# Moving two activation tensors by 128 and 384 bytes in SBUF, with everything behind them 512 bytes lower

## The reference, cut to what matters

```python
for layer in range(DEPTH):                       # first stack
    x = x + 0.5 * swiglu_ffn(rms_norm(x, ffn1_norm[layer]), w_gu, w_down)
    x = x + (even_mixer if layer % 2 == 0 else odd_mixer)(rms_norm(x, mix_norm[layer]), ...)
    x = x + memory_cross_attention(rms_norm(x, xa_norm[layer]), rms_norm(mem, ...), ...)
    x = x + 0.5 * swiglu_ffn(rms_norm(x, ffn2_norm[layer]), w_gu, w_down)
for l in range(DEPTH):                           # second stack
    x = x + 0.5 * rmsnorm(swiglu(rmsnorm(x, w_pre), w_gu, w_down), w_post)
    x = x + rmsnorm(merged(diff_attention, mlstm) @ w_out, w_mix_post)
    x = x + 0.5 * rmsnorm(swiglu(...), w_post)
```

## The kernel before, in words

| tensor | before | remainder by 256, by 512 | after | remainder by 256, by 512 |
|---|---|---|---|---|
| raw | 16512 | 128, 128 | 16512 | 128, 128 |
| a | 33056 | 32, 288 | 32928 | 160, 160 |
| b | 49696 | 32, 32 | 49312 | 160, 160 |
| x | 66272 | 224, 224 | 65760 | 224, 224 |
| score | 141024 | 224, 224 | 140512 | 224, 224 |
| hmid | 161568 | 32, 288 | 161056 | 32, 288 |
| w_hi | 163680 | 96, 352 | 163168 | 96, 352 |
| w_lo | 188256 | 96, 352 | 187744 | 96, 352 |

## Time and profile before

### The profile page before, as it was taken

The page is one execution under the profiler, slowest core; times in us unless marked ns, Lnnn a source line. Parts: engine busy times, 40 slices in busy tenths (PEclk is TensorE's granted clock), DMA queues, the critical chain, the costliest instruction groups (busy, mean ns, idle before and its releaser), DMA issues.

```text
span 2668.7 us, 51716 instructions
## 1 busy us (share of the span) xinstructions
PE 2587.6 (97%) x18604; PEld 2380.8 (89%) x18604; DVE 1919.6 (72%) x3131; ACT 1502.3 (56%) x2579; POOL 202.0 (8%) x280
## 2 busy tenths in 40 slices
PE   8999799999999999999999999999999999999998
PEld 7998689999999799999998998989989989988997
DVE  7777676778777586777777667777787776676876
ACT  6556556556555656556555555655565565555554
POOL 0001001000000101000000170000000004300000
PEclk9999899999999999999999999999999999999999
DMA  7654244665554254554654553445545545435553
GB/s 265 205 189 135 79 143 144 231 204 185 190 189 158 96 166 138 186 188 165 206 188 136 190 163 105 158 158 189 189 158 189 188 143 174 135 114 171 174 189 110
DMA packets 122821, 445.80 MB, mean 167 GB/s; under 512 B 13688, under 2 KB 14712, under 8 KB 122688
## 3 DMA queue, kind: packets, MB, share of 16 engines
q1 hardware_dynamic: 120816, 436.79, 49.4%
q0 software_dynamic: 1872, 7.17, 0.7%
HBM read 442.86 MB, written 1.05 MB: 166 GB/s over the span
## 4 chain that ended last, share of the span: by engine, by line
PE 92%; DVE 5%; ACT 2%; issue 1%; DMA 0%; SPq 0%; DVEq 0%; ACTq 0%
PE bank L459 91%; DVE w_lo L1473 1%; PE bank L810 1%; DVE rt L1701 1%; DVE z L1539 1%; ACT w_hi L1039 0%; DVE rt L1495 0%; DVE x L1532 0%; DVE a L1500 0%; ACT score L1273 0%; DVE rstd_x L1492 0%; DMA x<-in_x_dram 0%; ACT L1247 0%; DMA raw<-in_stream_dram 0%; DVE z L1645 0%
## 5 line engine op out<-in xcount | busy, mean ns | idle before, releaser
L459 PE MATMUL bank<-a,w_hi 128*128 128x256 f32 (+1 forms) x5360 | 1329.9, 328 | 40.6 <-DVE a L1500 37.9
L1473 DVE TENSOR_TENSOR w_lo<-raw,w_hi 128x1024 fp32r<-128x1024 f32 x829 | 1014.1, 1227 | 279.0 <-ACT w_hi L1039 278.6
L459 PE MATMUL bank<-a,w_lo 128*128 128x256 f32 x3736 | 1008.7, 281 | 0.0
L459 PEld LDWEIGHTS bank<-a,w_hi 128*128 128x128 f32 x5360 | 890.1, 190 | 130.7 <-issue 46.7
L1039 ACT CAST w_hi<-raw 128x1024 fp32r<-128x1024 f32 x829 | 858.3, 1047 | 40.5 <-DMA raw<-in_stream_dram 37.2
L459 PE MATMUL bank<-b,w_hi 128*128 128x256 f32 (+1 forms) x4096 | 845.0, 299 | 4.2 <-DVE b L1500 3.1
L459 PEld LDWEIGHTS bank<-a,w_lo 128*128 128x128 f32 x3736 | 707.9, 189 | 17.2
L459 PEld LDWEIGHTS bank<-b,w_hi 128*128 128x128 f32 x4096 | 651.5, 188 | 41.8 <-issue 3.6
L459 PE MATMUL bank<-b,w_lo 128*128 128x256 f32 x2400 | 653.9, 278 | 0.0
L459 PEld LDWEIGHTS bank<-b,w_lo 128*128 128x128 f32 x2400 | 450.6, 188 | 5.7
L1082 ACT COPY pt<-bank 128x256 f32<-128x256 f32 x176 | 65.3, 371 | 220.3 <-PE bank L459 220.3
(11 more groups left out here) (185 smaller groups left out, 2146.7 us busy)
## 6 DMA issues: line engine op xcount, KB each, us to landing
raw<-in_stream_dram SPq DMA_DIRECT2D x829, 512.0 KB, 3.3
z<-in_biasc_dram POOLq DMA_DIRECT2D x6, 512.0 KB, 4.6
z<-in_biasa_dram POOLq DMA_DIRECT2D x3, 512.0 KB, 4.6
x<-in_x_dram SPq DMA_DIRECT2D x2, 512.0 KB, 7.4
v<-in_mem_dram POOLq DMA_DIRECT2D x2, 512.0 KB, 6.4
out_dram<-x SPq DMA_DIRECT2D x8, 128.0 KB, 1.9
con<-in_con_dram POOLq DMA_DIRECT2D x1, 912.0 KB, 7.1
vec<-in_vec_dram POOLq DMA_DIRECT2D x1, 417.0 KB, 5.6
```

Of the source, the lines that this page charges most:

```text
L459: return nc.tensor.matmul(out, lhsT, rhs, start=start, stop=stop, skip_group_check=shared)
L1473: return nc.vector.tensor_tensor(out, a, hi.bitcast(F32), ALU.subtract)
```

## The change

Three of the four filler tensors are made smaller or taken out: `gap_a` from 160 to 16 bytes (32 with the rounding), `gap_b` from 256 bytes to nothing, `gap_x` from 192 bytes to 48 (64 with the rounding). `a` moves down by 128 bytes, `b` by 384, and `x` and everything declared behind it by 512. `gap_w` stays. `raw` stays where it is.

```diff
         raw = sb("raw", [P, RAW, D])
-        sb("gap_a", [P, 40])
-        a_two = sb("a", [P, C, 2, T], F32R)
-        sb("gap_b", [P, 64])
-        b_two = sb("b", [P, C, 2, T], F32R)
+        sb("gap_a", [P, 4])
+        a_two, b_two = sb("a", [P, C, 2, T], F32R), sb("b", [P, C, 2, T], F32R)
         a_hi, a_lo = a_two[:, :, 0, :], a_two[:, :, 1, :]
         b_hi, b_lo = b_two[:, :, 0, :], b_two[:, :, 1, :]
-        sb("gap_x", [P, 48])
+        sb("gap_x", [P, 12])
         x = sb("x", [P, C, T])
```

## The result

The changed kernel takes 2695.58 us (median of four runs, 2693.89 to 2697.03) against 2675.03 us (the three runs named before and a fourth): a ratio of 1.008, with a 95% interval of 1.0062 to 1.0098. The forecast was 2674 with a range of 2660 to 2693. So a change that adds no instruction and moves none costs 0.8%.

What follows compares the result with a forecast made beforehand. TensorE's matmul rate and its few waits for the norm bound the kernel. All terms summed to 0 against the profiled 2670.8 us; centred on the runs' median of 2674.6, the forecast was 2674, range 2660 to 2693.

Steps and rivals of the forecast that it cites:

- What bounds the kernel: Whole span: time depends only on TensorE's matmul rate and its few waits for the norm; TensorE busy 97%.
- x and everything behind it, 512 bytes: Tensors from x on, moved against raw, a and b: no step depending on 512 bytes, taken as 0.
- a and b by 128 and 384 bytes: TensorE's matmuls reading a or b: between 18.7 us lost and 37.5 us gained, value taken 0.
- Rival 1: Moving operand and weights collide: down tiles 18.7 us (2693), mixers and cross attention at most 32 more (2725); chance 0.13.
- Rival 2: Feed-forward pairs: present distance is the bad one, they rise to the fast pace, 37.5 us gained, 2637; chance 0.12.
- Rival 3: Clock or paces fall differently across the span: 2680 or 2668; chance 0.05 beyond 0.2%, shared evenly.
- VectorE and ScalarE: Their operations on a and b beside hmid and sil: 0.2 us on the path at 6 ns each, taken as 0.
- The rule that was weighed: SBUF contention only at the VectorE and GpSimd port pair: addresses play no part, sum 0; the prediction did not lean on it.

Runs made afterwards that it cites:

- weights following: The changed kernel with weight tensors w_hi and w_lo 128 bytes higher, a and b left in place: 2671.3 us against 2672.97, ratio 0.9994.
- the first two experiments: Changed kernel, w_hi and w_lo 128 bytes higher: ratio 0.9994. Kernel before, x and everything behind it including weights 128 bytes lower: ratio 1.0079.

## Why the prediction was wrong

**What bounds the kernel** was read rightly: the loss is in how fast TensorE takes its matmuls, for the most part at full clock (at most 4.2 of the 23.3 us are longer half clock).

**x and everything behind it, 512 bytes: 0.** Right. The kernel with weights following keeps x and all up to hmid at the changed kernel's places and is at 0.9994 of the kernel before.

**a and b by 128 and 384 bytes: 0.** This is the step that failed. Its fact was right: 256 bytes make no difference in that kernel. Its conclusion was not. It took two places that are alike modulo 256 as evidence on all addresses ("it is nearest to the rows that test an address"), though the text itself said that a period of exactly 256 was left and that nothing in the trace stood there. A test that is blind to the question got the weight of an answer. The square of the first two experiments shows what stands in its place: the distance between moving operand and weights modulo 256, worth 12.1 ns per down chunk. The text's other premise, that "the address does not choose between them here; something in the queue's history does", was half of the answer: the start chooses between two paces, and the distance decides whether there is a fast one to choose.

**Rival 1** named what came: the distance, the chunk as the place, and nearly the price. That the two reads collide, as it has it, is not shown. The down chunks were priced at 18.7 us and lost 17.0; mixers and cross attention at up to 32 and lost some 10 (the 12.0 less 2.0 of down tiles), up to 2.4 of it by the clock. Not in its price was the pairs' gain of 5.6 us, nor that some of the mixers' chunks have the weights as the moving operand. Those got faster: of 437 such chunks 140 took 338 to 344 ns before and 267 after. Its sum would have been 2693 to 2725; 2695.6 is what came. It had a chance of 0.13. Two paces of one form, 4% apart, were in the trace, and they should have been read as "this engine's pace is fragile", not as "the address does not choose".

**Rival 2** (the pair rises to 0.340) happened at about a seventh of its price, 5.6 of 37.5 us, and was outweighed. At distance 32 to 64 the pair is 2 to 4 ns shorter.

**Rival 3** played a small part in the profiled executions: 8.4 us more at half clock, at most 4.2 of 23.3 us. It can't be the cause, since blocks 2 to 5 lose 1.06 to 1.22 us each at full clock.

**The range** ended at 2693, the lower price of rival 1, so that the whole rest of that rival lay outside it.

**VectorE and ScalarE: 0.** Right: the remainder of b takes 424 ns again, the multiply into hmid 426.

```profile
L1570 DVE TENSOR_TENSOR hmid<-sil,hmid 128x256 f32<-128x256 f32 x176 | 75.0, 426 | 5.8
L1471 DVE TENSOR_TENSOR b<-hmid,b 128x256 fp32r<-128x256 f32 x132 | 56.0, 424 | 45.7 <-ACT b L1092 45.7
```

**The rule that was weighed.** The Trainium skill (SBUF — State Buffer, Who interferes with whom) has two read ports for TensorE, one for the moving operand and one for the weights, and says "PE and ACT never wait on anyone". On the other engines the runs agree: the paces with all of them idle are those of the whole kernel, within 3 ns. But neither that section's ports nor its rule has what was measured: one and the same chain of matmuls takes 0.340 to 0.360 us per chunk by where its moving operand starts. The measurement decides. That the two reads disturb each other is the reading that fits; the runs show that their distance matters, and do not show the conflict itself.

## What to carry to other kernels

Where TensorE is busy all the time and loads new weights for every matmul, compare the distance from start to start of one form across the whole trace: if one form has two paces a few per cent apart, the layout is a parameter, and moving either tensor by 32 or 128 bytes is a cheap thing to try. Filler tensors that nobody reads may be carrying time, so measure before tidying them; and a natural experiment in a trace counts only for the shifts that it contains.

## What was not expected of the hardware

With fp32r operands (the rounded float32 of this kernel) and a new weight load for each matmul, three matmuls of 256 columns take 0.340, 0.3467, 0.3533 or 0.360 us in many of the batches with TensorE alone at full clock (2.4 GHz). These are 16 cycles apart: 0.340 us is 816 cycles, 0.3533 is 848. A batch settles into its pace within some four chunks and then keeps it to the nanosecond; at other distances it repeats a pattern of eight chunks (352, 361, 355, 355, 365, 352, 356, 364 ns at distance 208). In a grid of 8 by 8 places of activations and w_lo in steps of 32 bytes only three cells gave a chunk of 0.340: distances of w_hi and w_lo of 192 and 192, 192 and 64, 64 and 192. The last of them is a place at which the whole kernel's chunks take 0.3569, so such a grid shows what is possible, not what a kernel will get.
